# Attention with the causal mask written into PSUM by ScalarE, keys scaled by minus the score scale, and meta copies once per output group

## What is computed

```python
scale = (QK_NOPE + QK_ROPE) ** -0.5          # 192 ** -0.5
def attend(qn, qr, qpos, kn, kr, vv, kpos):
    s = einsum('bqhd,bkhd->bhqk', qn, kn) + einsum('bqhd,bkd->bhqk', qr, kr)
    s = s * scale
    s = where(kpos <= qpos, s, -inf)
    p = softmax(s, axis=-1)
    return einsum('bhqk,bkhd->bqhd', p, vv)
```

## Time and profile before

| | |
|---|---|
| Three runs | 1549.93, 1550.31, 1551.9 us; median 1550.31 |
| The profiled execution | 1549.37 us |
| Its span, first to last instruction | 1547.6 us |
| Mean granted TensorE clock, share of full | 0.996 |
| Attention stage in it | about 350 to 645 us |
| PE, DVE, ACT, POOL busy, share of the span | 98%, 68%, 46%, 50% |

### The profile page before, as it was taken

One profiled execution on the slowest core, in us unless ns is written; L12 is line 12 of the kernel. 1 busy time (PEld: TensorE's weight loads), 2 busy tenths in 40 slices (PEclk: granted clock), 3 DMA queues, 4 the chain that ended last, 5 costly groups with the idle time before them and its releaser, 6 DMA issues.

```text
span 1547.6 us, 22730 instructions
## 1 busy us (share of the span) xinstructions
PE 1517.4 (98%) x7919; PEld 1307.4 (84%) x7919; DVE 1051.6 (68%) x1729; ACT 716.0 (46%) x1445; POOL 781.3 (50%) x686
## 2 busy tenths in 40 slices
PE   9999999999999999899999999999999999999997
PEld 8999998878888889788887888788888888888885
DVE  5856516256878778777778789765565677747676
ACT  5232211245656555566664554444444445444542
POOL 7534444134767766953321425776666135405653
PEclk9999999999999999999999999999999999999999
DMA  6444622226556545798878642454444696535666
GB/s 219 113 138 127 181 55 62 68 63 191 167 166 173 163 131 171 236 338 310 313 283 298 238 165 94 149 177 150 150 150 150 218 380 229 192 110 192 195 197 150
DMA packets 225796, 280.64 MB, mean 181 GB/s; under 512 B 21400, under 2 KB 148224, under 8 KB 225696
## 3 DMA queue, kind: packets, MB, share of 16 engines
q1 hardware_dynamic: 224688, 275.69, 54.8%
q0 software_dynamic: 1008, 3.67, 1.3%
HBM read 180.63 MB, written 98.66 MB: 180 GB/s over the span
## 4 chain that ended last, share of the span: by engine, by line
PE 81%; DVE 10%; issue 2%; ACT 2%; DMA 2%; POOL 2%; SPq 0%; DVEq 0%; ACTq 0%; POOLq 0%
PE ps L2981 19%; PE ps L2972 16%; PE ps L825 7%; PE ps L884 6%; PE ps L2842 5%; PE ps L1801 3%; PE ps L2918 3%; PE ps L840 2%; PE ps L856 2%; PE ps L1717 2%; PE ps L1739 2%; PE ps L458 1%; DVE pTlo L2020 1%; PE ps L1769 1%; PE ps L1786 1%
## 5 line engine op out<-in xcount | busy, mean ns | idle before, releaser
L2981 PE MATMUL ps<-dw_hi,df_hi 128*128 128x512 f32 x448 | 174.5, 389 | 1.6 <-DVE dw_lo L3568 1.6
L2981 PE MATMUL ps<-dw_lo,df_hi 128*128 128x512 f32 x448 | 174.3, 389 | 0.0
L2981 PE MATMUL ps<-dw_hi,df_lo 128*128 128x512 f32 x448 | 174.3, 389 | 0.0
L178 POOL TENSOR_TENSOR ring<-stage,zero 128x512 fp32r<-128x512 f32 (+2 forms) x75 | 83.7, 1116 | 150.8 <-DMA stage<-w_in 47.9
L3563 DVE TENSOR_TENSOR df_lo<-df_raw,df_hi 128x512 fp32r<-128x512 f32 x112 | 114.2, 1020 | 49.6 <-ACT df_hi L3259 48.5
L3568 DVE TENSOR_TENSOR dw_lo<-dw_raw,dw_hi 128x512 fp32r<-128x512 f32 x96 | 80.6, 840 | 43.8 <-ACT dw_hi L3268 26.4
L3259 ACT ACTIVATE df_hi<-df_raw 128x512 fp32r<-128x512 f32 x112 | 70.3, 627 | 71.8 <-DMA df_raw<-d_f 71.6
L180 POOL TENSOR_TENSOR ring<-stage,ring 128x512 fp32r<-128x512 f32 (+2 forms) x75 | 100.5, 1340 | 5.9
L2981 PEld LDWEIGHTS ps<-dw_hi,df_hi 128*128 128x128 f32 x448 | 84.1, 188 | 19.5 <-DVE df_lo L3563 2.0
L2981 PEld LDWEIGHTS ps<-dw_lo,df_hi 128*128 128x128 f32 x448 | 84.1, 188 | 17.5
L2981 PEld LDWEIGHTS ps<-dw_hi,df_lo 128*128 128x128 f32 x448 | 84.1, 188 | 17.4
(11 more groups left out here) (543 smaller groups left out, 4536.8 us busy)
## 6 DMA issues: line engine op xcount, KB each, us to landing
df_raw<-d_f SPq DMA_DIRECT2D x112, 256.0 KB, 2.7
d_f<-fa SPq DMA_DIRECT2D x105, 256.0 KB, 2.1
dw_raw<-w_mlp_down SPq DMA_DIRECT2D x96, 256.0 KB, 3.0
landA<-w_mlp_up SPq DMA_DIRECT2D x52, 256.0 KB, 3.2
stage<-w_in SPq DMA_DIRECT2D x40, 256.0 KB, 2.7
stage<-w_out SPq DMA_DIRECT2D x28, 256.0 KB, 5.3
xt<-x SPq DMA_DIRECT2D x8, 512.0 KB, 6.9
d_xT<-xdT SPq DMA_DIRECT2D x8, 512.0 KB, 3.3
```

The source lines that it names most:

```text
L178: pool.tensor_tensor(hi, src, k.zero[:, 0:1].broadcast_to([P, width]), ALU.add).then_inc(k.sem(fam + "_hi"), 1)
L2981: mm = pe.matmul(ps[:, base + t, :], F_AT[q % SLOTS][a][:, P * t:P * t + P], W_AT[q % SLOTS][b][:, :], start=(fresh and (a, b) == (0, 0)), ...
```

## The change

The score scale moves into the keys: ACT and DVE evacuate them times -SCALE, and `krT` is made times -SCALE too. PSUM then holds the negative of the scaled scores, DVE takes the minimum, and that minimum is the bias of exp itself, which has scale -1. The multiplication behind the maximum is gone.

The mask matmul is gone. ACT writes the mask (0, and +1e30 for keys ahead) from a bf16 row `mask_row` into the bank that holds the block's last columns (`fill`, 144 to 400 columns wide), and the first product of that tile adds to it (`start=not masked`). `fill(b + 2)` stands behind exp of block b on ACT, and waits for it (`a_exp`); PE waits for `a_fill` before the masked tile, which is now the second tile of a block with several. GpSimd makes `mask_row` at the start of the stage, and ACT waits for that and does the first two fills before its first evacuation. Blocks 5 and 7 lie at other columns, and block 7's lowest tile (256 columns) has a first product with its 256 keys twice, over the whole of bank 1.

DVE's subtraction covers piece 0 whole, and the copies to rows 64 and 32 are made once per output group: both by ACT, 16x512 each (`meta`), behind a wait for the lows (`a_t_lo`). The meta product is the last of `weigh`, and waits for them (`a_t_meta`).

```diff
@@ scores, PE
-            d0, d1 = n - P, n
-            for i, (c0, c1) in enumerate(tiles):
-                if b == NT - 1 and i == len(tiles) - 1:
+            if len(tiles) > 1:
+                tiles[:2] = tiles[1::-1]
+            for c0, c1 in tiles:
+                if b == NT - 1 and c0 == 0:
                     pe.wait_ge(sem("a_exp"), NT * h + b)
...
-                pe.matmul(out, qT[u][0][:, q], kT[u][0][:, c0:c1], start=True, stop=False)
-                lo, hi = max(c0, d0), min(c1, d1)
-                if lo < hi:
-                    pe.matmul(flat[:, s0 + lo:s0 + hi], k.mask_b[:, :], k.ident_b[:, lo - d0:hi - d0], start=False, stop=False)
...
+                masked, whole = c1 == n, b == NT - 1 and c0 == 0
+                if masked:
+                    pe.wait_ge(sem("a_fill"), NT * h + b + 1)
+                if whole:
+                    pe.matmul(ps[:, 1, :].rearrange("p (a b) -> p a b", a=2), qT[u][0][:, q],
+                              kT[u][0][:, 0:c1].unsqueeze(1).broadcast_to([P, 2, c1]), start=True, stop=False, skip_group_check=skip)
+                else:
+                    pe.matmul(out, qT[u][0][:, q], kT[u][0][:, c0:c1], start=not masked, stop=False, skip_group_check=skip)
@@ weigh, PE
-            pe.wait_ge(sem("a_t_dup"), NT * h + 4 * g + 4)
-            pe.matmul(ps[:, bank, :], v[0][:, u, NT, :], pT[0][:, 0, :], start=True, stop=False)
...
+            pe.wait_ge(sem("a_t_meta"), 2 * h + g + 1)
+            pe.matmul(ps[:, bank, :], v[0][:, u, NT, :], pT[0][:, 0, :], start=False, stop=True).then_inc(sem("a_o"), 1)
@@ high, meta, exp, fill, ACT
-                if p0 == 0:
-                    act.wait_ge(sem("a_t_hi"), NB * h + i + 1)
-                    act.activation(pT[0][64:64 + META, 0, own], pT[0][0:META, 0, own].bitcast(F32), ACT.Copy).then_inc(sem("a_t_dup"), 1)
...
+        def meta(h, g):
+            act.wait_ge(sem("a_t_lo"), NB * h + (first_batch[4] if g == 0 else NB))
+            act.activation(pT[0][64:64 + META, 0, :], pT[0][0:META, 0, :].bitcast(F32), ACT.Copy)
+            act.activation(pT[0][32:32 + META, 0, :], pT[1][0:META, 0, :].bitcast(F32), ACT.Copy).then_inc(sem("a_t_meta"), 1)
...
+            if b + 2 < NT or more:
+                act.wait_ge(sem("a_exp"), NT * h + b + 1)
+                fill((b + 2) % NT)
+
+        def fill(b):
+            c1 = start(b) + width(b)
+            c0 = max(start(b), (c1 - 1) // 512 * 512)
+            act.activation(flat[:, c0:c1], k.mask_row[:, 400 - (c1 - c0):400], ACT.Copy).then_inc(sem("a_fill"), 1)
@@ late, ACT
                 if b == 6:
+                    meta(h, 0)
                     out(h, 0)
@@ start of the stage, ACT
-        act.wait_ge(sem("a_v_set"), 2)
+        act.wait_ge(sem("a_v_set"), 5)
+        act.wait_ge(sem("qro_step0"), 2 * NT)
+        for b in range(2):
+            fill(b)
@@ DVE
-            dve.tensor_reduce(mx[:, b:b + 1], flat[:, s0:s0 + n], AX.X, ALU.max).then_inc(sem("a_mx"), 1)
-            dve.wait_ge(sem("a_mx"), NT * h + b + 1)
-            dve.tensor_scalar(nb[:, b:b + 1], mx[:, b:b + 1], -SCALE, None, ALU.mult).then_inc(sem("a_nb"), 1)
+            dve.tensor_reduce(least[:, b:b + 1], flat[:, s0:s0 + n], AX.X, ALU.min).then_inc(sem("a_nb"), 1)
...
-                if p0 == 0:
-                    dve.tensor_tensor(pT[0][32:32 + META, 0, own], ps[0:META, turn_bank(b, i, more), 0:P], pT[0][0:META, 0, own].bitcast(F32), ALU.subtract)
```

More of the change, by code:

```diff
@@ L1042, in on_scalar @@
             elif n < 12:
-                act.activation(k.krT[:, META + c0:META + c0 + 512], src, ACT.Copy).then_inc(sem("lat_hi"), 1)
+                act.activation(k.krT[:, META + c0:META + c0 + 512], src, ACT.Copy, scale=-SCALE).then_inc(sem("lat_hi"), 1)
             else:
@@ L1800, in weigh @@
                 for a, b in PASSES:
-                    mm = pe.matmul(ps[:, bank, c0:512], v[a][:, u, j, :], pT[b][:, j + 1, c0:512], start=False, stop=(j == last and a == 1))
-            mm.then_inc(sem("a_o"), 1)
+                    pe.matmul(ps[:, bank, c0:512], v[a][:, u, j, :], pT[b][:, j + 1, c0:512], start=(j == 0 and (a, b) == (0, 0)), stop=False)
+            pe.wait_ge(sem("a_t_meta"), 2 * h + g + 1)
+            pe.matmul(ps[:, bank, :], v[0][:, u, NT, :], pT[0][:, 0, :], start=False, stop=True).then_inc(sem("a_o"), 1)
         def scan_start(b):
@@ L1913, in piece @@
             for src, dst in evacs(n, u, piece_bank(n) if bank is None else bank):
[L1914 removed]
+                act.activation(dst[0], src, ACT.Copy, scale=-SCALE if PIECE[n][0] == "k" else 1.0).then_inc(sem("a_e_hi"), 1)
         def values(i, n):
@@ L1928, in late @@
                 if first:
-                    exp(h, b)
+                    exp(h, b, more)
                     if more:
@@ L1960, in next_early @@
             piece(h + 1, 1 - u, 4)
+            meta(h, 1)
             exp(h + 1, 2)
@@ L1988, in on_scalar @@
         weighted_high(act, k, 0, PROJ)
+        meta(HEADS - 1, 1)
         out(HEADS - 1, 1, LATE_OUT)
@@ L2014, in low @@
                 dve.wait_ge(sem("a_t_hi"), NB * h + i + 1)
-                own = slice(P * (b % 4), P * (b % 4) + P)
-                keys = 1 if p0 == 0 else 0
-                if p0 == 0:
-                    dve.tensor_tensor(pT[0][32:32 + META, 0, own], ps[0:META, turn_bank(b, i, more), 0:P], pT[0][0:META, 0, own].bitcast(F32), ALU.subtract)
-                hi, lo = (x[:, p0 + keys:p0 + np_, own] for x in pT)
-                dve.tensor_tensor(lo, ps[:, turn_bank(b, i, more), P * keys:P * np_].rearrange("p (a b) -> p a b", b=P), hi.bitcast(F32),
+                hi, lo = (x[:, p0:p0 + np_, P * (b % 4):P * (b % 4) + P] for x in pT)
+                dve.tensor_tensor(lo, ps[:, turn_bank(b, i, more), 0:P * np_].rearrange("p (a b) -> p a b", b=P), hi.bitcast(F32),
                                   ALU.subtract).then_inc(sem("a_t_lo"), 1)
@@ L2064, in late @@
                     normalise(h, b - 1)
-                most(h, b)
+                smallest(h, b)
                 if b == NT - 1 and not more:
@@ L2084, in next_early @@
         def next_early(h, u, last=False):
-            most(h + 1, 0)
+            smallest(h + 1, 0)
             normalise(h, NT - 1)
@@ L2088, in next_early @@
             low(h, NT - 2)
-            most(h + 1, 1)
+            smallest(h + 1, 1)
             piece(h + 1, 1 - u, 3)
             low(h, NT - 1)
-            most(h + 1, 2)
+            smallest(h + 1, 2)
             normalise(h + 1, 0)
@@ L2104, in on_vector @@
         for b in range(3):
-            most(0, b)
+            smallest(0, b)
             if b:
```

42 lines of the change are left out of this document (25 added, 17 removed).

## The result

The changed kernel takes 1554.88 us (median of 14 runs, 1551.9 to 1557.93), the kernel before beside it 1550.03 (14 runs): ratio 1.0027, 95% interval 1.0019 to 1.0036. It is slower by 4 to 5 us, where 2.5 were forecast. The profiled execution of the changed kernel took 1555.09 us with a span of 1553.0, against 1549.37 and 1547.6.

What follows compares the result with a forecast made beforehand. TensorE, busy 286.16 of 295 us, bounds the attention stage, its waits for the ScalarE-VectorE chain deciding. Heads 0 to 6 +2.0, start +0.6, last head -0.1: +2.5 us, giving 1552.6 us, range 1546 to 1559.

Steps and rivals of the forecast that it cites:

- The mask matmul, -0.13 us: TensorE, blocks 1 to 7: each removed mask product saves 0.13 us, -0.91 a head; block 7's wider product adds 0.12.
- ACT's and DVE's work: Attention stage: ScalarE's sum rises 29 us to about 201 of 295, no bound by itself; VectorE loses 18 us.
- The new wait, 1.43 us: First output group: TensorE's last product waits 1.43 us per head for ScalarE's meta copies, bounds 1.0 and 1.8.
- what follows starts 0.1 before its end: ScalarE's queue in block 6: the instruction behind a meta copy of 0.62 us starts 0.1 us before that copy ends.
- The gap before block 6's transposes, -0.42: TensorE's 0.72 us wait for VectorE's low of block 5 shrinks by 0.42 a head, bounds 0 and -0.72.
- The fill before block 1, +0.07: Next head's block 1, one tile without cover: TensorE waits for the fill, +0.07 us, bounds 0 and 0.4.
- Start, +0.6, and last head, -0.1: First head's block 2 scores wait for a fill, +0.6 us (0.4 to 1.5); last head -0.1 despite a 2.0 stall.
- The sum: Heads 0 to 6 lose 0.29 us each, +2.0; with start and last head the whole kernel loses 2.5 us.
- Faster: Rival: stall 1.0 us, VectorE's lighter chain shortens gaps; -0.75 a head, 1545.6 us; needs stall under 0.9; chance 0.20.
- Slower, by an ACT that is late: Rival: fills delay ScalarE's high copies at head boundaries, VectorE gives nothing back; +1.14 a head, 1558.8 us; chance 0.28.
- The clock falls behind the new wait: Rival: after 1.43 us pauses TensorE's clock falls, block 7's scores take twice as long; 19 us more, 1571; chance 0.02.
- the slower side of 0.2%: Whole kernel: measurement tells about 0.2%, 3 us, from no change; chances slower than 1553.4 us 0.41, same 0.40, faster 0.19.

Runs made afterwards that it cites:

- early copies: Changed kernel with the first output group's two meta copies moved ahead of block 6's exp on ScalarE: 1543.02 us, ratio to the kernel before 0.9955.
- mask part alone: Kernel before with ScalarE fills instead of the mask matmul, keeping the maximum, its scaling and per-block meta copies: 1553.30 us, ratio 1.0017.
- third copy: Changed kernel with one more 16x512 ScalarE copy in the first output group, to rows with zero weights: 1569.09 us, ratio to before 1.0121.
- scale part alone: Kernel before with the scale in the keys and the minimum as bias, mask still a TensorE product: 1548.24 us, ratio 0.9982.
- change without meta part: Changed kernel with per-block meta copies and the meta product first again, fills and scale kept: 1547.52 us, ratio to the kernel before 0.9985.
- meta part alone: Kernel before with only the once-per-group meta copies, behind exp and key piece in block 6, and meta product last: 1556.41 us, ratio 1.0037.

## Why the prediction was right, and where it was off

The forecast was 1552.6 us with a range of 1546 to 1559; measured were 1554.88. The mechanism was the forecast's: gains of some tenths per head against one new wait for the meta copies, eight times. One term was too small. Point by point:

**The mask matmul, -0.13 us: right.** Block 4 in the changed kernel, third head, first and third product of its first tile:

```profile
443.73 0.31 PE L1776 MATMUL ps<-kT0hi,qT0hi 128*128 128x328 f32 x1
...
444.03 0.31 PE L1778 MATMUL ps<-kT0hi,qT0lo 128*128 128x328 f32 x1
```

and in the kernel before, where the mask stands between them:

```profile
441.57 0.31 PE L1762 MATMUL ps<-kT0hi,qT0hi 128*128 128x328 f32 x1
...
442.00 0.32 PE L1767 MATMUL ps<-kT0hi,qT0lo 128*128 128x328 f32 x1
```

0.30 for 0.43 (the tile that holds the mask is the second one now, and takes 0.31 from 444.48 to 444.79). The check that the prediction named, 0.46 in block 5, fits no row, since block 5 is now two tiles of 392 columns (0.37 there); it should have named this block.

**ACT's and DVE's work: right in the parts.** Fills 27.6 us for 29; meta copies 0.63 us each for 0.62; DVE's sum went from 1051.6 to 1033.8, 17.8 for 18. ACT's sum rose by 22.4, not 29: 4.4 of that is in the rows of the high copies, of which two often follow each other directly now and share a row. So ACT is busy for about 194 us of the stage, not 201.

**The new wait, 1.43 us: the mechanism right, the term too small.** Counted from PE's start at 455.71 in the two timelines on top: exponential at +1.35 (forecast 1.35), fill at +2.49 (2.50), PE's last product before the wait at +2.72, so ready at +2.83 (2.83). Up to there the working holds to 0.01. Then the key piece is followed by the first copy after 0.47 (forecast 0.36), the second comes after another 0.64 (0.53), and PE starts at +4.51 (4.26). The step that was off is "what follows starts 0.1 before its end": that came from the exponential and its read the earlier trace rows, and the two copies don't do it, each starts when the one ahead has ended. That is 0.25. Another 0.11 is in the meta product itself: 0.34 to the next start (460.22 to 460.56) where the forecast has 0.23. Only 0.05 of it is the pause's; with early copies and no pause the same product takes 0.29 (455.32 to 455.61), so 0.06 is the price of its new place ahead of the transposes, a term that the forecast put at nothing. In all 1.79 for 1.43, near the upper bound of 1.8. Over seven heads that is 2.5 us. The recorded waits are 1.50 to 1.54 in seven heads and 1.94 in the last (2.0 forecast).

**The gap before block 6's transposes, -0.42: right in the mean.** From the transposes of block 5 to those of block 6 the seven heads took 0.80, 0.75, -0.21, 0.58, 0.37, 0.55 and 0.42 us less than before, 0.47 in the mean. From the last product of block 0 to the transposes, where the forecast had 0.72 falling to about 0.3, these heads went from 0.68 to 0.31 in the mean. The third head lost some instead:

```profile
463.19 1.63 DVE L2034 TENSOR_SCALAR prob<-prob,stat 128x912 f32<-128x912 f32 x1
...
466.62 1.12 PE L1797 MATMUL ps<-ident,prob 128*128 128x128 f32 x8 [0.51 <-DVE pTlo L2040]
```

DVE's normalisation of block 6 took 1.63 us there; the same operation took 0.70 in the kernel before, in the same head.

**The fill before block 1, +0.07: about 0.2.** From the transposes of block 6 to those of block 7 the heads took 0.06 more than before although a mask (0.13) is gone from the stretch. Directly: between the last transpose of block 6 and the first product of block 1 stood 0.03 us, and now 0.19 to 0.24 (six heads).

**Start, +0.6, and last head, -0.1: right but for the clock.** PE waits at block 2 of the first head as forecast, and then something happens that wasn't (the row that answers to the earlier trace rows, and the 400-column products behind it):

```profile
365.32 0.45 PE L1776 MATMUL ps<-kT0hi,qT0hi 128*128 128x400 f32 x1 [1.17 <-ACT ps L1924]
365.59 0.52 PE L1777 MATMUL ps<-kT0lo,qT0hi 128*128 128x400 f32 x1
365.91 0.54 PE L1778 MATMUL ps<-kT0hi,qT0lo 128*128 128x400 f32 x1
```

```profile
366.00:368.00 2.00, 2.00 (x10) 1.90 (x8) 0.82 (x3) 0.34 (x2) 0.00 (x0) 0.50 0.51 129
```

The products stand 0.33 apart instead of 0.18 and the granted clock is 0.50, 1.2 GHz, from 365.6 to 369.0. From the first of these products to the transposes of block 1 it is 5.40 us, and 3.82 to 3.87 in the four kernels with the same fills whose clock held there: 1.5 us lost. These transposes start 1.70 later than before; in those four kernels they start 0.5 to 0.8 later, for the forecast 0.6. The same comes back behind the last wait of the stage, which answers to the earlier trace rows:

```profile
645.44 2.12 PE L1797 MATMUL ps<-ident,prob 128*128 128x128 f32 x9 [1.25 <-DVE pTlo L2040]
...
646.00:650.00 4.00, 4.00 (x16) 3.21 (x15) 2.68 (x4) 2.17 (x4) 3.92 (x4) 0.64 1.02 388
```

Nine transposes take 2.12 us for 1.27. Without it the last head would be near the -0.1.

**The sum.** Per head (0 to 6) the trace lost 0.61 us where 0.29 were forecast; the difference is about the wait's 0.36. With the clock at both ends the output projection starts at 654.3 instead of 647.2, 7.1 later for the forecast 2.5. 1.7 of it come back in the remaining 900 us (span 5.4 longer), and where wasn't looked into. But that is one pair of executions, and in the medians the clock hardly enters: its mean over all executions is 0.9956 with the change (14) and 0.9958 in the kernel before (15, beside the first experiments), while one stretch of 3.4 us at 0.50 is 0.0011 of a mean. So in its other executions the kernel before has such stretches about as often. The median's excess over the forecast, 2.3 us (4.8 for 2.5), then matches the wait's 2.5 us, and the two falls weigh on the profiled pair alone. This is my estimate from means recorded to three decimals; it isn't shown stretch by stretch.

**The rivals.** *Faster* needed a wait under 0.9: it was 1.79. *Slower, by an ACT that is late:* its sign came and its consequence did not. The high copies of block 6 start 2.13 to 2.25 us behind PE's transposes (1.13 to 1.22 before), and 0.5 us later than before in the mean if counted from block 5's transposes; yet PE's gap before block 6's transposes shrank as forecast. So ACT is late, and it doesn't decide there. The mask part alone comes nearest to that case: 2.6 us slower without any wait for meta copies, with a gap that did not shrink. That DVE's relief by the other two parts hides this in the change is my reading, and not shown.

*The clock falls behind the new wait:* not at 1.5 us, 1.00 in all eight heads, and the warning of the Trainium skill that stood with it (TensorE: Matmul & The Clock Gate, "HAM oscillation — how this bites in real kernels"), that pauses between bursts of matmuls let the clock fall, did not come true there. It did 0.64 us further on, with the third copy, where the trace agrees with it. With a chance of 0.02 that rival had been taken too lightly for how near it stood, and its refutation was weaker than it looked: it rested on one wait of 1.85 us in one execution. The same wait in the kernel with the scale part alone:

```profile
637.70 2.15 PE L1788 MATMUL ps<-ident,prob 128*128 128x128 f32 x9 [1.79 <-DVE pTlo L2020]
```

The transposes behind it take 2.15 us for 1.27, and the granted clock is 0.50 from 637.7 to 641.0. It also fell there behind 1.82 us (change without meta part) and 1.89 (mask part alone). So that one pause could not carry so small a chance. What the runs do show is that none of the eight new waits brought a fall, nor did the first seven waits for the copies, about 1.35 us each, with the meta part alone; the eighth there, 2.03 us, did.

The median was slower by 0.27 to 0.31%, on the slower side of 0.2%, with the lower end of the interval just below it.

## What to carry to other kernels

When a consumer is moved behind a producer on another engine, count the producer's place in that engine's queue, not its length: here 1.3 us of copies per head cost 12 us over the eight heads in one place and nothing four instructions earlier, where the engine was waiting for something else. Split a change into its parts before judging it: two of these three parts are gains of 2.4 and 4.6 us (the second once its copies stand early), and the third alone is a loss of 2.6, though it takes most work from the busiest engine. And price a chain of small instructions by rows of the same kind (same source memory, same neighbours), since an overlap seen between two of another kind was missing between these. Last, one trace in which the clock held, or fell, behind a pause says little of the next execution: look at several traces, and at the mean clock of all runs.

## What the runs showed of the hardware

**Behind longer pauses the clock fell more often, but length alone doesn't decide.** Pauses of 1.5 us (1.94 in the last head) before the meta product left the granted clock at 1.00 in eight heads of eight; pauses of 2.15 brought it to the lower level in six heads of seven, 2.54 in the last head too. Filling over half of the pause with bf16 products of zeros kept it at 1.00. Elsewhere shorter pauses did it in some traces and not in others (one profiled execution of each kernel). At block 2 of the first head PE waits for a fill in eight kernels. The clock fell behind this wait in four of them, each time after 1.17 us, as in the changed kernel; it held in the other four, after 1.16, 1.17, 1.17 and 1.36. The first of these is the version with early copies:

```profile
365.97 0.42 PE L1776 MATMUL ps<-kT0hi,qT0hi 128*128 128x400 f32 x1 [1.16 <-ACT ps L1924]
366.23 0.34 PE L1777 MATMUL ps<-kT0lo,qT0hi 128*128 128x400 f32 x1
```

In the last head it held behind 1.85 us (kernel before) and fell behind 1.79, 1.82, 1.89 and, in the changed kernel, 1.25; with early copies it held there behind 1.2. What decides is open.

**ScalarE's copies of 16 rows within SBUF follow each other without overlap,** 0.64 us apart at 0.63 each, while the read of the accumulator starts 0.1 before the end of the exponential that reads PSUM. Whether it is the memory that matters or the 16 rows wasn't tested.

**The same DVE operation took 0.70, 0.93 and 1.63 us** (normalising block 6's 912 columns in the third head: before, mask part alone, changed kernel). GpSimd works beside it in all three, in the slowest case with a subtraction over 512 columns (1.28 us) where the others have 256; that it is the cause was not tested.
